# Router logits by token: which operand is stationary, and who copies the last tile

## The reference, cut to what matters

```python
def hier_moe(h, w_group, b_group, w_router, b_router, w_gate, w_up, w_down):
    hf = h.astype(jnp.float32)
    pg = jax.nn.softmax(hf @ w_group + b_group, axis=-1)          # 4 groups
    g_val, g_idx = lax.top_k(pg, 1)
    logits_all = jnp.einsum('btd,gde->btge', hf, w_router) + b_router   # 4 x 8 experts
    ...
    e_val, e_idx = lax.top_k(pe, TOP_K)                           # the best two in the best group
    ...
    a = jnp.einsum('btd,edf->btef', h, w_gate)
    u = jnp.einsum('btd,edf->btef', h, w_up)
    z = jax.nn.silu(a) * u * combine[..., None].astype(a.dtype)
    return jnp.einsum('btef,efd->btd', z, w_down).astype(h.dtype)
```

## Time and profile before

| | |
|---|---|
| Median of 3 runs | 622.52 us (622.03 to 624.54) |
| The profiled execution: its own time | 623.2 us |
| Its span, first to last instruction | 621.4 us |
| Mean granted TensorE clock | 0.913 |
| TensorE busy | 492.7 us (79%) |
| TensorE weight loads busy | 264.1 us (43%), beside the products |
| VectorE busy | 225.2 us (36%) |
| ScalarE busy | 156.7 us (25%) |
| GpSimd busy | 114.5 us (18%) |
| Moved by DMA | 172.99 MB, 278 GB/s in the mean |

### The profile page before, as it was taken

How to read it: one execution, slowest core, us unless ns; L and a number is a source line. 1 busy time by engine, 2 the same in 40 slices (tenths; PEclk the granted TensorE clock), 3 DMA queues, 4 the chain that set the end, 5 groups by cost and what they waited for, 6 DMA issues and landing times.

```text
span 621.4 us, 8713 instructions
## 1 busy us (share of the span) xinstructions
PE 492.7 (79%) x2920; PEld 264.1 (43%) x2921; DVE 225.2 (36%) x572; ACT 156.7 (25%) x339; POOL 114.5 (18%) x175
## 2 busy tenths in 40 slices
PE   1869999999987999984345776448887988788994
PEld 0448787788633344432331332113433344333442
DVE  0342543142686259899670111010111021111144
ACT  1211434532756203222001111010122121111233
POOL 5030002000084440011010121120222222222200
PEclk9969999999999799988557799688999899999998
DMA  8994864420492951215999599999999898999822
GB/s 276 399 349 184 283 239 162 177 73 0 186 373 57 410 129 68 88 50 218 366 420 330 220 414 420 419 421 419 420 400 408 348 419 320 410 416 362 306 89 85
DMA packets 48544, 172.99 MB, mean 278 GB/s; under 512 B 14776, under 2 KB 24048, under 8 KB 33134
## 3 DMA queue, kind: packets, MB, share of 16 engines
q1 hardware_dynamic: 39034, 150.74, 62.2%
q0 software_dynamic: 9136, 21.76, 9.6%
q10 hardware_dynamic: 340, 0.09, 0.1%
HBM read 162.07 MB, written 27.71 MB: 305 GB/s over the span
## 4 chain that ended last, share of the span: by engine, by line
PE 61%; DMA 17%; DVE 11%; issue 6%; ACT 2%; SPq 2%; POOL 0%; POOLq 0%; DVEq 0%; ACTq 0%
PE PB L1658 17%; PE PB L1933 15%; DMA wB<-in_w_up 9%; PE PB L1958 7%; PE PB L1828 6%; DMA ada_m<-in_w_ada 4%; PE PB L1595 2%; PE PB L1982 2%; DMA ada<-in_w_ada 2%; PE PB L1727 1%; PE PB L1797 1%; PE PB L1912 1%; PE PB L1756 1%; PE PB L1670 1%; PE PB L1980 1%
## 5 line engine op out<-in xcount | busy, mean ns | idle before, releaser
L1933 PE MATMUL PB<-wA,XT 128*32 128x512 f32 x480 | 115.0, 633 | 43.8 <-DMA wB<-in_w_up 23.8
L1933 PE MATMUL PB<-wB,XT 128*32 128x512 f32 x480 | 114.9, 634 | 0.0
L1658 PE MATMUL PB<-hT,win 128*128 128x256 f32 (+1 forms) x448 | 103.9, 392 | 2.0 <-DVE hT L1066 2.0
L1658 PEld LDWEIGHTS PB<-hT,win 128*128 128x128 f32 x448 | 86.0, 194 | 22.5 <-issue 9.4
L1933 PEld LDWEIGHTS PB<-wA,XT 128*32 128x32 f32 x480 | 37.3, 116 | 115.0 <-issue 110.4
L1958 PE MATMUL PB<-wA,zT 128*32 128x512 f32 x240 | 55.8, 606 | 5.7 <-ACT zT L946 5.7
L1504 DVE SCALAR_TENSOR_TENSOR z<-silu_g,w_now,PB 128x256 f32<-128x256 f32 x15 | 7.2, 481 | 145.8 <-ACT silu_g L944 145.8
L1958 PE MATMUL PB<-wB,zT 128*32 128x512 f32 x240 | 55.8, 608 | 0.0
L1828 PE MATMUL PB<-wout,yT 128*128 128x512 f32 x112 | 48.8, 593 | 0.0
L944 ACT ACTIVATE silu_g<-PB 128x256 f32<-128x256 f32 x15 | 5.7, 383 | 135.1 <-PE PB L1933 135.1
L1510 DVE TENSOR_TENSOR yo<-PB,gate_row 128x512 f32<-128x512 f32 x15 | 10.4, 692 | 70.7 <-PE PB L1958 65.7
(11 more groups left out here) (427 smaller groups left out, 686.0 us busy)
## 6 DMA issues: line engine op xcount, KB each, us to landing
wB<-in_w_gate SPq DMA_DIRECT2D x24, 1024.0 KB, 15.5
wB<-in_w_up SPq DMA_DIRECT2D x24, 1024.0 KB, 19.6
wB<-in_w_down SPq DMA_DIRECT2D x24, 1024.0 KB
ada<-in_w_ada POOLq DMA_DIRECT2D x12, 1024.0 KB, 7.5
ada<-in_w_ada SPq DMA_DIRECT2D x8, 1024.0 KB, 11.9
wA<-in_w_gate SPq DMA_DIRECT2D x8, 1024.0 KB, 15.4
wA<-in_w_up SPq DMA_DIRECT2D x8, 1024.0 KB, 18.6
wA<-in_w_down SPq DMA_DIRECT2D x8, 1024.0 KB
```

The lines of the kernel that those rows point to most:

```text
L1658: last = pe.matmul(B[(q % 2) * 2 + h][:, 0:cn], win[:, n % 3, k, col:col + P], hT[:, k, c0:c0 + cn], start=(k == 0), stop=(k == KD - 1))
L1933: last = pe.matmul(B[2][32 * g:32 * g + 32, :], XT[:, k, 32 * g:32 * g + 32], gu[:, :, k, :], start=(k == 0), stop=(k == KD - 1))
```

## The change

The tokens' transposed tile becomes the stationary side and the router weights stream past it: for each tile eight products with up to 128 stationary columns and 36 moving ones, so that the logits come out with tokens on partitions. `LGT`, the addition to it and the five transposes back go. The bias is loaded to all partitions (`br`), behind the router weights, and VectorE adds it as it moves the logits from PSUM into `LG`: one addition for the first three tiles, one for the samples, one for the last tile. The logits of the first three tiles stand before the last tile's transposes on TensorE, those of the samples and of the last tile behind them.

ScalarE makes both copies of the last tile's `h2T`. On VectorE the two halves of the last `first_output` are taken apart: the product stands ahead of the wait for the last logits, the addition behind the last tile's bias addition. The waits of SyncE for the router's semaphores are merged into one, for the last logits, in front of the second narrow pair.

```diff
--- before.py
+++ after.py
@@ -174,7 +174,7 @@
         h2 = row("h2", [P, 2, D], "r", 81920)
         h2T = row("h2T", [P, KD, NT], "r", 49152)
         wr = row("wr", [P, KD, NG + NE], "r", 94208)
-        LGT = row("LGT", [NG + NE, NT], "r", 90112)
+        br = row("br", [P, NG + NE], "r", 90112)
         rs = row("rs", [P, 264], "r", 96448)
         gb = row("gb", [P, D], "r", 67584)
 
@@ -232,7 +232,6 @@
         rden = small("rden", [P, 2, NH])
         sv = small("sv", [P, 8, 2])
         rT = small("rT", [P, TT + 1, 2])
-        brt = small("brt", [NG + NE, 1])
         bn = small("bn", [P, 2, 6])
         mv = small("mv", [P, 2])
         st1 = small("st1", [P, 4])
@@ -344,8 +343,7 @@
         var_ready, std_ready, norm_ready, xhat_ready, x1_ready, h2_ready = (sem(n) for n in (
             "var_ready", "std_ready", "norm_ready", "xhat_ready", "x1_ready", "h2_ready"))
         h2_stored, x1_stored = [sem("h2_stored0"), sem("h2_stored1")], sem("x1_stored")
-        h2T_ps, h2T_v, h2T_a, lgT_ps, lgT_ready, lg_ps = (sem(n) for n in (
-            "h2T_ps", "h2T_v", "h2T_a", "lgT_ps", "lgT_ready", "lg_ps"))
+        h2T_ps, h2T_v, h2T_a, lg_ps = (sem(n) for n in ("h2T_ps", "h2T_v", "h2T_a", "lg_ps"))
         top_ready, top_exp, hot_ready, rank_ps, rows_ready, slot_ready = (sem(n) for n in (
             "top_ready", "top_exp", "hot_ready", "rank_ps", "rows_ready", "slot_ready"))
         place_ps, idx_made, count_ps, steps_ready = (sem(n) for n in (
@@ -400,8 +398,6 @@
                 if n == 3:
                     sp.dma_start(kc[:, :, :], A["cache_k"][0].rearrange("b w k d -> w b (k d)")).then_inc(kv_in, 16)
                     sp.dma_start(vc[:, :, :], A["cache_v"][0].rearrange("b w k d -> w b (k d)")).then_inc(kv_in, 16)
-                    sp.dma_start(brt[0:NG, :], A["b_group"].rearrange("a g -> g a")).then_inc(kv_in, 16)
-                    sp.dma_start(brt[NG:NG + NE, :], A["b_router"][0].rearrange("g (e a) -> (g e) a", a=1)).then_inc(kv_in, 16)
 
                     for o, a in ((8, "cache_k"), (9, "cache_v")):
                         sp.dma_start(O[o][0, :, 0:WIN - 1].rearrange("b w k d -> b w (k d)"),
@@ -463,6 +459,8 @@
             sp.dma_start(wr[:, :, 0:NG], pair_rows(A["w_group"][0])).then_inc(wr_in, 16)
             for g in range(NG):
                 sp.dma_start(wr[:, :, NG + g * EPG:NG + (g + 1) * EPG], pair_rows(A["w_router"][0, g])).then_inc(wr_in, 16)
+            sp.dma_start(br[:, 0:NG], A["b_group"].broadcast_to((P, NG))).then_inc(wr_in, 16)
+            sp.dma_start(br[:, NG:NG + NE], A["b_router"].rearrange("a g e -> a (g e)").broadcast_to((P, NE))).then_inc(wr_in, 16)
             for i, t, n in MIX:
                 if i == TT:
                     sp.wait_ge(rows_ready, 3)
@@ -480,9 +478,8 @@
             sp.wait_ge(x1_stored, 16 * (3 * TT + 1))
             load_b(0, 0)
             load_b(0, 1)
-            sp.wait_ge(lgT_ps, 2)
+            sp.wait_ge(lg_ps, TT + 1)
             load_b(1, 0)
-            sp.wait_ge(lg_ps, 1)
             sp.wait_ge(h2_stored[0], 16 * (TT // 2 + 1))
             sp.wait_ge(h2_stored[1], 16 * (TT // 2))
             load_b(1, 1)
@@ -914,6 +911,9 @@
                                bias=st1[0:n, 3:4]).then_inc(xhat_ready, 1)
 
             def copy_h2T(i, t, n):
+                if i == TT:
+                    act.wait_ge(h2T_ps, 2 * i + 1)
+                    act.activation(h2T[:, 0:4, t * P:t * P + n], B[4][:, :].rearrange("p (k m) -> p k m", m=P)[:, :, 0:n], ACT.Copy).then_inc(h2T_a, 1)
                 act.wait_ge(h2T_ps, 2 * i + 2)
                 act.activation(h2T[:, 4:8, t * P:t * P + n], B[5][:, :].rearrange("p (k m) -> p k m", m=P)[:, :, 0:n], ACT.Copy).then_inc(h2T_a, 1)
 
@@ -1295,31 +1295,35 @@
                 dve.scalar_tensor_tensor(out=h2[0:n, i % 2, :], in0=h2[0:n, i % 2, :], scalar=st1[0:n, 2:3], in1=shift,
                                          op0=ALU.mult, op1=ALU.add).then_inc(h2_ready, 1)
 
-            def first_output(i, t, n):
-
-                dve.wait_ge(xhat_ready, i + 1)
-                link(dve.tensor_tensor(x_tok[0:n, t, :], x_tok[0:n, t, :], mod[0:n, 3, :], ALU.mult))
-                dve.tensor_tensor(x_tok[0:n, t, :], x_tok[0:n, t, :], mod[0:n, 4, :], ALU.add).then_inc(x1_ready, 1)
+            def first_output(i, t, n, parts=(0, 1)):
+
+                if 0 in parts:
+                    dve.wait_ge(xhat_ready, i + 1)
+                    link(dve.tensor_tensor(x_tok[0:n, t, :], x_tok[0:n, t, :], mod[0:n, 3, :], ALU.mult))
+                if 1 in parts:
+                    dve.tensor_tensor(x_tok[0:n, t, :], x_tok[0:n, t, :], mod[0:n, 4, :], ALU.add).then_inc(x1_ready, 1)
 
             dve.wait_ge(rows_ready, 1)
-            for i in range(TT + 2):
+            for i in range(TT + 1):
                 if i == TT - 1:
                     dve.wait_ge(rows_ready, 2)
-                if i <= TT:
-                    residual(*MIX[i])
-                    modulate2(*MIX[i])
-                    if i < TT - 1:
-                        first_output(*MIX[i])
-                    elif i == TT:
-                        first_output(*MIX[TT - 1])
-                else:
-                    copy_h2T(*MIX[TT])
-                    first_output(*MIX[TT])
-
-            dve.wait_ge(lgT_ps, 1)
-            dve.tensor_scalar(LGT[:, 0:T - P], B[6][0:NG + NE, 0:T - P], brt[:, 0:1], None, ALU.add).then_inc(lgT_ready, 1)
-            dve.wait_ge(lgT_ps, 2)
-            dve.tensor_scalar(LGT[:, T - P:NT], B[7][0:NG + NE, 0:P + NS], brt[:, 0:1], None, ALU.add).then_inc(lgT_ready, 1)
+                residual(*MIX[i])
+                modulate2(*MIX[i])
+                if i < TT - 1:
+                    first_output(*MIX[i])
+                elif i == TT:
+                    first_output(*MIX[TT - 1])
+
+            link(dve.memset(LG[:, TT, :], 0.0))
+            dve.wait_ge(wr_in, 16 * 7)
+            dve.wait_ge(lg_ps, TT)
+            step(dve.tensor_tensor(LG[:, 0:TT - 1, :], B[6][:, 0:(TT - 1) * (NG + NE)].rearrange("p (t e) -> p t e", e=NG + NE),
+                                   br[:, :].rearrange("p (t e) -> p t e", t=1).broadcast_to((P, TT - 1, NG + NE)), ALU.add))
+            step(dve.tensor_tensor(LG[0:NS, TT, :], B[6][0:NS, TT * (NG + NE):(TT + 1) * (NG + NE)], br[0:NS, :], ALU.add))
+            first_output(*MIX[TT], parts=(0,))
+            dve.wait_ge(lg_ps, TT + 1)
+            step(dve.tensor_tensor(LG[:, TT - 1, :], B[7][:, 0:NG + NE], br[:, :], ALU.add))
+            first_output(*MIX[TT], parts=(1,))
 
             def per_tile(v, n):
 
@@ -1337,10 +1341,6 @@
                 link(dve.tensor_tensor(out, c_, per_tile(col[:, 6, :], n), ALU.is_equal))
 
 
-            link(dve.memset(LG[:, TT, :], 0.0))
-            dve.wait_ge(lg_ps, 1)
-            step(dve.tensor_copy(LG[:, 0:TT, :], B[6][:, 0:TT * (NG + NE)].rearrange("p (t e) -> p t e", e=NG + NE)))
-            step(dve.tensor_copy(LG[0:NS, TT, :], B[6][0:NS, TT * (NG + NE):(TT + 1) * (NG + NE)]))
             settle()
             link(dve.tensor_reduce(col[:, 0, :], LG[:, :, 0:NG], AX.X, ALU.max))
             dve.tensor_tensor(gt[:, 0, :, :], LG[:, :, 0:NG], per_tile(col[:, 0, :], NG), ALU.subtract).then_inc(top_ready, 1)
@@ -1688,7 +1688,7 @@
             def cached_keys():
 
                 pe.wait_ge(vt_ready, 4)
-                pe.wait_ge(kv_in, 16 * 4)
+                pe.wait_ge(kv_in, 16 * 2)
                 for b in range(NS):
                     last = pe.transpose(B[6 + b // 4][:, (b % 4) * P:(b % 4 + 1) * P], kc[:, b, :], ident[:, :])
                     if b % 4 == 3:
@@ -1851,10 +1851,12 @@
                     if k % 4 == 3:
                         last.then_inc(h2T_ps, 1)
 
-            def logits(bank, c0, cn):
+            def logits(i, t, n):
+                out = B[7][:, 0:NG + NE] if i == TT else B[6][0:n, t * (NG + NE):(t + 1) * (NG + NE)]
                 for k in range(KD):
-                    last = pe.matmul(B[bank][0:NG + NE, 0:cn], wr[:, k, :], h2T[:, k, c0:c0 + cn], start=(k == 0), stop=(k == KD - 1))
-                last.then_inc(lgT_ps, 1)
+                    last = pe.matmul(out, h2T[:, k, t * P:t * P + n], wr[:, k, :],
+                                     start=(k == 0), stop=(k == KD - 1))
+                last.then_inc(lg_ps, 1)
 
             pe.wait_ge(rs_ready, 2)
             for c in range(2):
@@ -1871,16 +1873,13 @@
             transpose_h2(*MIX[TT - 2])
             project_out(*MIX[TT], groups=(1,))
             transpose_h2(*MIX[TT - 1])
-            pe.wait_ge(wr_in, 16 * 5)
-            logits(6, 0, T - P)
+            pe.wait_ge(wr_in, 16 * 7)
+            for i in range(TT - 1):
+                logits(*MIX[i])
             transpose_h2(*MIX[TT])
-            pe.wait_ge(h2T_v, TT + 1)
-            pe.wait_ge(h2T_a, TT + 1)
-            logits(7, T - P, P + NS)
-            pe.wait_ge(lgT_ready, 2)
-            for t, n in TILES:
```

(5 more changed lines are left out.)

## The result

The changed kernel took 617.08 us in the median (616.33 to 618.34, 4 runs) against 622.46 for the kernel before: the ratio is 0.991 [0.988, 0.994]. In a later session it took 618.41 against 623.4, 0.993 [0.991, 0.996]. So it is some 5 us faster, where 2 us slower was forecast (624.5, range 620.6 to 627.0). The profiled execution of the changed kernel took 618.34 us with a span of 616.6 and a mean granted clock of 0.913, the same clock as before.

The account below looks back on a forecast made before the run. The prediction took the chain of waits through the router on VectorE, then the expert steps, as the bound. Router +4.1 us and first-step gap -2.1 gave +2.0: 622.52 becomes 624.5 us, range 620.6 to 627.0.

Parts of the forecast that it names:

- the first expert step: TensorE's 6.47 us gap after the step's first products: starting 4.1 us later, it shrinks by 2.1 us; bounds 0 and -5.8.
- B: Rival: the first step's gap at 337.98 does not shrink, the whole +4.1 us is paid, 626.6 us; chance 0.20.
- Rival C: With the loop moved, the first step's gap nearly goes: 4.1 - 5.8 = -1.7 us, so 620.8; chance 0.12.
- the transfer of the packet: 16 KB instruction packet crossing the DMA engines in the first step's gap: 3.1 us falls to 0.93 with an emptier queue.
- The logits block: First three tiles' router logits on TensorE: 48 load-bound records at 0.233 us and 1.2 GHz, 11.2 us from 275.46.
- the clock's allowance: 0.5 us (between 0 and 2) off the reduction's +4.6 us, in case the clock falls later in another execution; leaves +4.1.
- Rival A: Narrow router products bring TensorE's clock back at 281.4: router -1.2 us, step gap unchanged, 621.3 us; chance 0.16.
- The place blocks: TensorE's place products, 4.66 us of nearly the logits' shape, stayed at clock 0.50 to their end: evidence against rival A.
- The tail of the router: On TensorE after the last copies: sample logits 1.3 us, to 289.9, then the last tile's logits 3.7 us, to 293.6.
- ScalarE's copies of 0.60 us: Both copies of the last tile's h2T move to ScalarE at 0.60 us each; the second ends at 289.25.
- the last store of `x1`: In SyncE's queue: waits for x1 ready at 295.0, reached before at 295.29, cover 0.3 us; weights still start about 301.5.
- The prediction's last sign: If the reduction is 4 us late and the end not later, something behind it has slack the chain doesn't show.

Follow-up runs that it names:

- the changed kernel with 43 more: Changed kernel with 43 more TensorE wait instructions ahead of the expert loop, after the rank products; 622.31 us, 1.000 of the kernel before.
- the changed kernel with 127 more: Changed kernel with 127 more TensorE wait instructions ahead of the expert loop, in places where TensorE waits anyway; 622.62 us, 1.000 of the kernel before.
- after +171, idle: Changed kernel with 171 more TensorE wait instructions ahead of the loop, in places where TensorE waits anyway; 624.77 us, 1.004 of the kernel before.
- the edited queue: Kernel before, with SyncE loading the second later unit's gate and up weights ahead of the first's down weights: 616.65 us; with 85 idle-time TensorE waits too: 616.69.
- the changed kernel with 171: Changed kernel with 171 more TensorE wait instructions, half ahead of the count products, half after the rank products; 622.81 us, 1.001 of the kernel before.

## Why the prediction was wrong

**The step that failed is the first expert step.** The prediction said: "The weights keep their start, so a first step that is 4.1 us later meets an emptier queue: I take 3.1 - 0.93 = -2.1 us." It priced the gap of 6.47 us as time of TensorE, on a chain where each microsecond counts once, and gave its size as the only question: shrinks (forecast), stays (B), nearly goes (C). The gap moved behind the down products, and its size hardly mattered. Its price was in what the down products release. The prediction even read that the steps' progress "releases the weight transfers", but followed the queue only to 301.48 and never asked which of TensorE's instructions the loads at 353.83 waited for. Had it asked, the answer stood in the trace of before: the loads go 2.0 us after the end of the down products, and the transfers ran at 110 GB/s for the 8 us ahead of that. It also took 370.63 for the start of a wait, where it is SyncE's issue of a load. Rival C had the cause half right ("With the loop moved") and still counted it on TensorE, to 620.8. As far as the runs show, the change came out faster by a side effect, the number of instructions that it adds, and not by the router's rework.

The gap also costs more than itself there. Behind the standstill of 6.47 us the granted clock of the kernel before was 0.65 in the mean (last but two of the columns of rows 3), and the down products took 4.93 us on the chain instead of 3.64:

```profile
344.40:351.80 7.40, 7.33 (x42) 3.15 (x42) 0.69 (x1) 0.98 (x2) 0.00 (x0) 0.65 0.36 148
```

In the changed kernel the second step's gate and up products pay instead (9.84 us on the chain, 7.26 before), where a wait for weights follows anyway.

The Trainium skill (Runtime: NRT & Kernel Launch, "Instruction fetch mechanics") says that a taken branch out of the fetched window stops execution for a fetch. That the gaps move when nothing but the number of instructions ahead of the loop is changed agrees with it (6.47 and 1.95, or 0 and 7.84, for the same code). So does the view of a single line, which also has the branches of TensorE's sequencer (PEldq; columns: shortest, median and longest ns, first and last start). Before, the branches ahead of the gate and up products:

```profile
L1925 PEldq COMPARE_BRANCH  x4: 85/288/7129, 328.9 to 335.9; - x4
```

After, those ahead of the down products:

```profile
L1947 PEldq COMPARE_BRANCH  x4: 66/273/5715, 340.9 to 343.0; - x4
```

One branch took 7.13 us before, from 335.9 to 343.1, so it outlasts the products (until 337.98) and makes 5.1 us of the gap of 6.47. After, one took 5.71 us, from 343.0 to 348.7, which is 3.7 us of the gap of 8.00; the register loads and branches of the next step fill the rest. Before, these run from 349.5 to 353.7, about half of them beside the down products (until 351.78).

The prediction took the transfer of the packet for the part that could shrink, and there it was wrong: the DMA queues of the changed kernel show the slow packet nowhere, and one in its gap, from 346 to 346.5 us, took 12.3% of 16 engines over 0.5 us, 0.98 us. So a branch of over 5 us is there without a slow packet. In both kernels the packet starts while the branch lasts (between 338 and 338.5 before), but in the changed kernel it is under a fifth of it.

```profile
q8 instruction: 1, 0.02, 12.3%
```

What else such a branch waits for isn't shown. Nor is every standstill one branch: in the changed kernel with 43 more, the 4 us lie between the check of a register load (337.8) and the next branch (342.0).

**The logits block was mis-sized.** Forecast were 11.2 us for 48 records and a reduction 4.6 later (4.1 with the clock's allowance). In the nine profiles of the new router the 48 records took 8.27 to 10.39 us. The longest, the changed kernel with 171 more in idle time, had the clock at 0.50 from their start: 0.216 each, so 0.233 was also a little high. The rest is the clock: in the changed kernel it fell 2.3 us into the block. Busy time by stretch of the changed kernel (columns as in rows 3):

```profile
276.00:276.50 0.50, 0.50 (x7) 0.50 (x6) 0.50 (x1) 0.00 (x0) 0.00 (x0) 1.00 0.00 0
...
277.00:277.50 0.50, 0.50 (x4) 0.50 (x4) 0.47 (x2) 0.00 (x0) 0.00 (x0) 0.50 0.00 0
...
284.30:289.00 4.70, 4.70 (x33) 4.43 (x32) 1.71 (x5) 1.88 (x2) 0.00 (x0) 0.50 0.75 288
```

From the samples' transposes to the reduction the kernel before took 15.99 us, and the four other profiles of the old router 16.73 to 17.33, 16.8 in the mean of five. The new router took 16.1 to 18.9, 17.3 in the mean of nine. So the rework cost about 0.6 us by these profiles, not 4.1: the single profile of before was the fastest of its five, since its second block of logits, the 2.04 us of the earlier trace rows, ran at 2.4 GHz. In the others that block met the lower clock and took 3.5 to 3.8. TensorE's timeline of the kernel before with 85 instructions in idle time has both of the old blocks:

```profile
274.49 5.35 PE L1858 MATMUL PB<-h2T,wr 128*36 128x384 f32 x16
285.32 3.84 PE L1858 MATMUL PB<-h2T,wr 128*36 128x136 f32 x16 [1.81 <-DVE h2T L1267]
```

An allowance for the clock belonged on both sides of the sum.

**Rival A** and its rule: the Trainium skill (TensorE: Matmul & The Clock Gate, "What's actually happening") says that activity releases the throttle. In five of the nine profiles of the new router the clock stayed at 0.50 through the samples' and the last tile's logits; in four it came back within them, between 286.1 and 290.2, as here in the changed kernel with 127 more:

```profile
287.00:288.00 1.00, 1.00 (x11) 1.00 (x11) 1.00 (x3) 0.70 (x1) 0.00 (x0) 1.00 1.01 410
```

So the clock can come back during the new router's products, but some five to nine microseconds later than A had it (281.4), and not in every execution. The place blocks, on which the argument against A rested, are no sure guide.

**What held.** The tail of the router: 16 sample and 16 last-tile records took 4.69 us on TensorE's timeline (5.0 forecast). ScalarE's copies of 0.60 us and the last store of `x1` went as said:

```profile
294.14 1.21 SPq L473 DMA_DIRECT2D x_dram<-x_tok  x1
...
300.19 0.34 SPq L411 DMA_DIRECT2D wB<-in_w_gate  x1
```

The store goes at 294.14 and the first weights at 300.19, both 1.2 to 1.3 us earlier than in the earlier trace rows, which is by how much the whole execution ran ahead. The prediction's last sign, a late reduction with an end that is not later, didn't come up in the changed kernel, whose reduction isn't late (290.44 against 290.48). But the slack that it speaks of is there, at the start of the steps: "after +171, idle" starts them 2.9 us later than "before" and its fourth step at 395.97 against 396.31, since TensorE waits for the weights in both.

## What to carry to other kernels

Where a loop is bound by transfers, price a stall by what it holds back, not by its length: find the instruction whose semaphore the next loads wait for, and ask on which side of it the stall lies. An in-order queue makes a load wait for everything ahead of it, so loads that are released earlier belong ahead of loads that are released later; here that was worth 6.7 us and made the kernel indifferent to the router and to the places of the gap that were tried. And an edit that changes the number of instructions ahead of a loop with branches can move the time on its own (3.5 us here), so a small gain or loss is put down to the edit only after the old code has been run at the new place.

## What the runs showed of the hardware

In the first pass of the expert loop a single branch of TensorE took up to 7.13 us (kernel before) or 5.71 us (changed kernel), where the median of its line's four was 0.29 and 0.27 us.

The standstill moves with the number of TensorE instructions ahead of the loop: 85 waits in idle time turned gaps of 6.47 and 1.95 us, ahead of and behind the down products, into 0 and 7.84. The number alone does not fix it: the same 85 behind the rank products gave 0 and 4.96, and with the edited queue, in idle time, 1.14 and 7.72; 256 more than before (the changed kernel with 171) did not bring back 6.47 and 1.95 but gave 2.5 and some 3. The two gaps together were 2.4 to 8.9 us.

The same kernel meets the drop of TensorE's clock at different points: in two executions of the changed kernel it fell at 276.6 and at 274.3 us of the span, after the same pause of 2.04 or 2.03 us ahead of the samples' transposes. In the nine profiles of the new router it fell between 274.1 and 276.6; in one of the five of the old router only after 283, with the same pause.
